# First-stage preparation of a two-block transformer kernel: parameters loaded in working layout, x on both partition halves

## The reference

```python
def rmsnorm(x, gain):
    y = x * rsqrt(mean(x * x) + EPS)
    return y * gain

def s5_mixer(u, lam, log_dt, b, c, d_skip, w_glu):      # 64 groups of 16 channels, 64 complex states each
    dt = exp(log_dt)
    a_bar = exp(lam * dt)
    b_bar = (a_bar - 1) / lam * b
    states = scan(a_bar, u @ b_bar)                     # along the 512 positions
    y = real(states @ c) + d_skip * u
    val, gate = split(gelu(y) @ w_glu)
    return val * sigmoid(gate)

def memory_cross_attention(h, m, w_q, w_kv, w_o):       # m = rmsnorm(mem) * g_mem
    kv = m @ w_kv                                       # 256 tokens, 256 key and 256 value columns
```

## Time and profile before

| what | us |
|---|---|
| median of three runs | 1854.55 |
| the profiled execution's own time | 1854.59 |
| its span, first to last instruction | 1852.8 |
| TensorE busy | 1814.2 |
| VectorE busy | 1144.7 |
| ScalarE busy | 838.7 |
| GpSimd busy | 734.2 |
| end of the load of x | 24.15 |
| first instruction of `rotate_in(0)` on VectorE | 53.29 |

### The profile page before, as it was taken

One profiled execution on the slowest core, in us unless ns is written; L12 is line 12 of the kernel. 1 busy time (PEld: TensorE's weight loads), 2 busy tenths in 40 slices (PEclk: granted clock), 3 DMA queues, 4 the chain that ended last, 5 costly groups with the idle time before them and its releaser, 6 DMA issues.

```text
span 1852.8 us, 24719 instructions
## 1 busy us (share of the span) xinstructions
PE 1814.2 (98%) x9727; PEld 1460.9 (79%) x9727; DVE 1144.7 (62%) x1684; ACT 838.7 (45%) x1361; POOL 734.2 (40%) x423
## 2 busy tenths in 40 slices
PE   7999999999999999999999999999999999999998
PEld 5778888888887688668888888887776768888886
DVE  8962435547475698853355474632636558787878
ACT  6852523333335435764323333353457464343444
POOL 1224343443424378543443443244245443324222
PEclk9999999999999999999999999999999999999999
DMA  6464452331412222003523414125120223415041
GB/s 169 89 149 101 117 156 69 114 114 46 137 46 75 69 92 91 24 24 109 165 68 108 120 46 137 46 83 153 57 69 24 80 92 113 128 54 169 13 137 46
DMA packets 200238, 171.29 MB, mean 92 GB/s; under 512 B 19258, under 2 KB 174346, under 8 KB 200058
## 3 DMA queue, kind: packets, MB, share of 16 engines
q1 hardware_dynamic: 197810, 165.93, 30.5%
q10 hardware_dynamic: 2312, 3.78, 0.6%
HBM read 162.58 MB, written 2.65 MB: 89 GB/s over the span
## 4 chain that ended last, share of the span: by engine, by line
PE 91%; DVE 3%; ACT 3%; issue 1%; DMA 1%; POOL 1%; SPq 0%; POOLq 0%; DVEq 0%; ACTq 0%
PE PS L2705 79%; PE PS L3067 2%; PE PS L3058 2%; PE PS L3077 2%; DMA xp<-in_x 1%; PE PS L2575 1%; PE PS L2618 1%; DVE taken L2393 1%; PE PS L3017 1%; PE PS L2984 0%; ACT probs_t L1481 0%; PE PS L2567 0%; PE PS L2627 0%; PE PS L2633 0%; ACT sq_junk L1138 0%
## 5 line engine op out<-in xcount | busy, mean ns | idle before, releaser
L783 POOL TENSOR_TENSOR w_lo<-raw,w_hi 128x2048 fp32r<-128x2048 f32 x92 | 430.1, 4675 | 604.2 <-ACT w_hi L1085 582.6
L2705 PE MATMUL PS<-xT_hi,w_hi 128*128 128x512 f32 (+1 forms) x1160 | 444.6, 383 | 3.1 <-DVE xT_lo L1922 2.0
L2705 PE MATMUL PS<-xT_lo,w_hi 128*128 128x512 f32 (+1 forms) x1160 | 441.8, 381 | 0.0
L2705 PE MATMUL PS<-xT_hi,w_lo 128*128 128x512 f32 (+1 forms) x1160 | 441.7, 381 | 0.0
L1085 ACT ACTIVATE w_hi<-raw 128x2048 fp32r<-128x2048 f32 x105 | 201.2, 1917 | 331.1 <-PE PS L2705 322.8
L2705 PEld LDWEIGHTS PS<-xT_hi,w_hi 128*128 128x128 f32 x1160 | 217.8, 188 | 50.0 <-issue 8.6
L2705 PEld LDWEIGHTS PS<-xT_lo,w_hi 128*128 128x128 f32 x1160 | 217.8, 188 | 42.2
L2705 PEld LDWEIGHTS PS<-xT_hi,w_lo 128*128 128x128 f32 x1160 | 217.9, 188 | 41.1
L790 POOL TENSOR_TENSOR w_lo<-dn_raw,w_hi 128x1024 fp32r<-128x1024 f32 (+1 forms) x46 | 123.4, 2703 | 262.5 <-ACT w_hi L1249 262.5
L2705 PE MATMUL PS<-w_hi,xT_hi 128*128 128x512 f32 (+1 forms) x560 | 220.2, 393 | 1.5 <-issue 1.5
L2705 PE MATMUL PS<-w_hi,xT_lo 128*128 128x512 f32 (+1 forms) x560 | 216.8, 387 | 0.0
(11 more groups left out here) (428 smaller groups left out, 2785.6 us busy)
## 6 DMA issues: line engine op xcount, KB each, us to landing
raw<-in_ffn_w_gate_up SPq DMA_DIRECT2D x88, 512.0 KB, 5.0
dn_raw<-in_ffn_w_down SPq DMA_DIRECT2D x22, 1024.0 KB, 7.6
raw<-in_w_up SPq DMA_DIRECT2D x32, 512.0 KB, 5.5
dn_raw<-in_w_down SPq DMA_DIRECT2D x16, 1024.0 KB, 8.0
raw<-in_dsa_w_in SPq DMA_DIRECT2D x28, 512.0 KB, 4.4
raw<-in_w_in SPq DMA_DIRECT2D x21, 512.0 KB, 4.9
raw<-in_s_w_glu SPq DMA_DIRECT2D x32, 256.0 KB, 4.9
raw<-in_dsa_w_o SPq DMA_DIRECT2D x8, 512.0 KB, 4.3
```

What stands on the lines that cost most here:

```text
L783: pool.tensor_tensor(w_lo[:, g % 2, :], raw[:, r % 2, :], f32(w_hi[:, g % 2, :]), ALU.subtract).then_inc(w_split, 1)
L2705: ins = mm(o, a if weights_stay else c, c if weights_stay else a, start=first and n == 0, stop=last and n == 2, skip_group_check=onto)
```

## The change

Parameters that were turned on the chip come from the host in the layout in which they are used (`laid_out`, a transposition and stacking of the arrays without arithmetic): lambda in one load, B as `b_n` and `b_s`, C as `c_n` and `c_s` (512 KB each), the gains as one 128x80 array, `w_kv` with 8 KB in a row per partition. The turns on TensorE and the copies on ScalarE for them go. Their signs change so that the state is kept conjugate: `rot` and `sign` change sign, `c_n` and `c_s` need no scaling, and `output_map` reads `pw_is` where it read `pw_i`.

x goes to 128 partitions, four positions of each chunk per partition (`xp[:, s, :]` for four `s`), in two loads of 64 partitions each. There are 4 squares of 128 partitions where there were 8 of 64, one inverse root in place of two, and all 8 scalings are ScalarE's, each still 64 partitions.

The order of the loads is log_dt, lambda, `mem`, `g_row`, B, x, the keys' half of `w_kv`, C, the values' half. ScalarE squares `mem` ahead of the two sines, and copies all of `memT` ahead of the squares of x. TensorE multiplies the first half of the keys ahead of the swap of B, and the rest behind it; the values' second half and `s5_lags(0)` move behind the turns of `u`. VectorE loses the three scalings, `pw_is` (now ScalarE's, behind the last square) and eight small instructions (memsets, the eighth power `r8` and the squared modulus of lambda, now GpSimd's), and makes `chunk_turns` ahead of `output_map(0)`. ScalarE makes `table(0)` behind `turned_rows`, where it stood ahead of `in_map_out(0)`.

```diff
 SyncE
-            for j, name in ((0, "s5_lambda_re"), (1, "s5_lambda_im")):
-                for half in range(2):
-                    sp.dma_start(nat_l[:, j, half, :], w[name][0]).then_inc(ld_lam, 16)
+            sp.dma_start(small[:, 1:3, :], w["s5_lambda"]).then_inc(ld_lam, 16)
+            sp.dma_start(mem[:, :, :], w["mem_2"].rearrange("(b p) d -> p b d", p=P)).then_inc(ld_mem, 16)
             sp.dma_start(g_row[:, :], w["norm_mix"][0:1, :]).then_inc(ld_rows, 16)
...
-            sp.dma_start(mem[:, :, :], w["mem_2"].rearrange("(b p) d -> p b d", p=P)).then_inc(ld_mem, 16)
-            sp.dma_start(xp[:, :, :], w["x"].rearrange("(c s) d -> c s d", s=CH)).then_inc(ld_x, 16)
...
+            for j, t in enumerate((b_n, b_s)):
+                sp.dma_start(t[:, :, :], w["s5_b"][:, j, :, :]).then_inc(ld_b, 16)
+            x_halves = w["x"].rearrange("(c f s) d -> f c s d", f=2, s=CQ)
+            for f in range(2):
+                sp.dma_start(xp[NC * f:NC * f + NC, :, :], x_halves[f]).then_inc(ld_x, 16)
+            sp.dma_start(w_kv[:, 0, :, :], w["w_xkv_2"][:, 0, :, :]).then_inc(ld_kvw, 16)
+            for j, t in enumerate((c_n, c_s)):
+                sp.dma_start(t[:, :, :], w["s5_c"][:, j, :, :]).then_inc(ld_c, 16)
+            sp.dma_start(w_kv[:, 1, :, :], w["w_xkv_2"][:, 1, :, :]).then_inc(ld_kvv, 16)
 GpSimd
+            pool.wait_ge(ld_lam, 16)
+            link(pool.tensor_tensor(small[:, 15, :], small[:, 1, :], small[:, 1, :], ALU.mult))
+            link(pool.tensor_tensor(small[:, 16, :], small[:, 2, :], small[:, 2, :], ALU.mult))
+            pool.tensor_tensor(small[:, 17, :], small[:, 15, :], small[:, 16, :], ALU.add).then_inc(const_set, 1)
...
+            pool.wait_ge(s5_ang, 1)
+            link(pool.tensor_tensor(r8[:, :], small[:, 8, :], small[:, 8, :], ALU.mult))
...
+            pool.wait_ge(s5_sq, CQ)
+            rsqrt(rstd[:, 0:CQ], ssq[:, 0:CQ], CQ, 1.0 / D).then_inc(s5_rstd, 1)
 ScalarE
-            square(0, 2)
-            mem_turned(0)
-            mem_turned(1)
-            square(2, 4)
-            mem_turned(2)
-            mem_turned(3)
+            for i in range(4):
+                mem_turned(i)
+            square(0, CQ - 1)
             act.wait_ge(s5_swap, 1)
             act.activation(b_s[:, 0:G // 2, :].rearrange("p g h -> p (g h)"), PS[:, 0, :], ACT.Copy)
             act.activation(b_s[:, G // 2:G, :].rearrange("p g h -> p (g h)"), PS[:, 7, :], ACT.Copy).then_inc(s5_bs, 1)
...
+            square(CQ - 1, CQ)
+            act.wait_ge(s5_pw, 1)
+            act.activation(pw_is[:, :, :], pw_i[:, :, :], ACT.Copy, scale=sign[:, 1:2]).then_inc(s5_pw_is, 1)
...
+            act.wait_ge(s5_rstd, 1)
+            for f in range(2):
+                for s in range(CQ):
+                    of = slice(NC * f, NC * f + NC)
+                    act.activation(u[:, :, CQ * f + s, :], xp[of, s, :].rearrange("p (g h) -> p g h", h=GH), ACT.Copy, scale=rstd[of, s:s + 1]).then_inc(s5_u, 1)
...
+            kv_copy(0)
             in_map_out(0)
-            turned_rows(0, 1)
-            kv_copy(0)
-            turned_rows(1, U_EARLY)
+            turned_rows(0, U_EARLY)
+            act.wait_ge(s5_u, CH)
+            table(0)
             lag_out(0)
 VectorE
+                if b == 0:
+                    dve.wait_ge(s5_bs, 1)
+                    dve.wait_ge(s5_pw_is, 1)
                 link(tt(in_im[:, :, :, :], over_k(b_s, b, CH), p_im, ALU.mult))
...
-            dve.wait_ge(s5_bs, 1)
-            dve.wait_ge(s5_skip, 1)
+            dve.wait_ge(s5_pw, 1)
             input_map(0)
-            dve.wait_ge(s5_nat_sb, 5)
+            chunk_turns()
+            dve.wait_ge(ld_c, 16 * 2)
             output_map(0)
-            chunk_turns()
-            dve.wait_ge(s5_rstd, 2)
-            for s in U_BY_DVE:
-                ts(u[:, :, s, :], xp[:, s, :].rearrange("p (g h) -> p g h", h=GH), rstd[0:NC, s:s + 1], None, ALU.mult).then_inc(s5_u_dve, 1)
             input_map(1)
 TensorE
+            def kv_keys(t):
+                for k in range(KT):
+                    if t == 0 and k % 2 == 0:
+                        pe.wait_ge(mem_t_sb, k // 2 + 1)
+                    ins = mm(PS[:, 4, MEM * t:MEM * t + MEM], w_kv[:, 0, k, P * t:P * t + P], memT[:, k, :], start=k == 0, stop=k == KT - 1)
+                return ins
+            pe.wait_ge(ld_kvw, 16)
+            kv_keys(0)
             pe.wait_ge(s5_bn, 1)
             pe.wait_ge(ld_rot, 16)
             for b in range(2):
                 ins = mm(PS[:, 7 * b, :], rot[:, 2 * P:3 * P], b_n[:, 32 * b:32 * b + 32, :].rearrange("p g h -> p (g h)"), start=True, stop=True)
             ins.then_inc(s5_swap, 1)
...
+            kv_keys(1).then_inc(kv_done, 1)
...
             s5_in_turn(0)
-            s5_lags(0)
-            kv_values(1).then_inc(kv_done, 1)
...
+            pe.wait_ge(s5_u, CH)
             u_turn(0, 3)
             pe.wait_ge(s5_int_sb, 1)
             u_turn(3, U_EARLY)
             pe.wait_ge(kv_sb, 1)
+            kv_values(1).then_inc(kv_done, 1)
+            pe.wait_ge(ld_c, 16 * 2)
+            s5_lags(0)
             pe.wait_ge(s5_ut_sb, 1)
             s5_in(0)
```

More of the change, by code:

```diff
@@ L768, in _ @@
             rsqrt(rstd[:, 32:34], ssq[:, 32:34], 2, 1.0 / D).then_inc(mem_rstd, 1)
-            for half in range(2):
-                rows = slice(CH // 2 * half, CH // 2 * half + CH // 2)
-                pool.wait_ge(s5_sq, rows.stop)
-                rsqrt(rstd[0:NC, rows], ssq[0:NC, rows], CH // 2, 1.0 / D, NC).then_inc(s5_rstd, 1)
+            pool.wait_ge(s5_ang, 1)
+            link(pool.tensor_tensor(r8[:, :], small[:, 8, :], small[:, 8, :], ALU.mult))
+            link(pool.tensor_tensor(r8[:, :], r8[:, :], r8[:, :], ALU.mult))
+            link(pool.tensor_tensor(r8[:, :], r8[:, :], r8[:, :], ALU.mult))
+            pool.wait_ge(s5_sq, CQ)
+            rsqrt(rstd[:, 0:CQ], ssq[:, 0:CQ], CQ, 1.0 / D).then_inc(s5_rstd, 1)
             def split_run(g0, n):
@@ L1775, in powers @@
                 link(tt(p, x, y[:, ::-1, :, :], ALU.mult))
-                link(tt(pw_i[:, :, lo + e:lo + e + n], p[:, 0, :, :], p[:, 1, :, :], ALU.add))
-            for lo, n, e in ((1, 1, 1), (1, 2, 2), (1, 4, 4)):
-                powers(lo, n, e)
-            link(ts(pw_is[:, :, :], pw_i[:, :, :], sign[:, 0:1], -1.0, ALU.mult, ALU.mult))
-            cycles = CH / (2 * np.pi)
-            link(ts(pt(10), pt(11), cycles, None, ALU.mult))
-            link(ts(pt(5).bitcast(I32), pt(11), cycles, None, ALU.mult))
+                return tt(pw_i[:, :, lo + e:lo + e + n], p[:, 0, :, :], p[:, 1, :, :], ALU.add)
+            link(powers(1, 1, 1))
+            link(powers(1, 2, 2))
+            powers(1, 4, 4).then_inc(s5_pw, 1)
             for side in range(2):
                 rows, gs = slice(GP * side, GP * side + GP), slice(G // 2 * side, G // 2 * side + G // 2)
-                link(stt(small[rows, 13, 0:G // 2], small[rows, 5, gs].bitcast(I32), -1.0, small[rows, 10, gs], ALU.mult, ALU.add))
+                link(stt(small[rows, 13, 0:G // 2], small[rows, 0, gs].bitcast(I32), -1.0, small[rows, 10, gs], ALU.mult, ALU.add))
             def chunk_turns():
@@ L1802, in output_map @@
                 gs = slice(GB * b, GB * b + GB)
-                p_re, p_im = (t[:, gs, 1:CH + 1].unsqueeze(3).broadcast_to([P, GB, CH, GH]) for t in (pw_r, pw_i))
+                p_re, p_im = (t[:, gs, 1:CH + 1].unsqueeze(3).broadcast_to([P, GB, CH, GH]) for t in (pw_r, pw_is))
                 if b >= 3:
@@ L2529, in _ @@
             ins.then_inc(s5_swap, 1)
-            pe.wait_ge(ld_c, 16 * 3)
-            for b in range(NB):
-                ins = tr(PS[:, 5 + b // 4, P * (b % 4):P * (b % 4) + P], nat_c[:, b, 0:2, :].rearrange("g a p -> g (a p)"), ident[:, :])
-            ins.then_inc(s5_nat, 1)
-            pe.wait_ge(mem_t_sb, 2)
-            for b in range(NB):
-                ins = tr(PS[:, 1 + b // 4, P * (b % 4):P * (b % 4) + P], nat_c[:, b, 1:3, :].rearrange("g a p -> g (a p)"), ident[:, :])
-            ins.then_inc(s5_nat, 1)
-            pe.wait_ge(mem_t_sb, 4)
-            pe.wait_ge(ld_kvw, 16)
-            for t in range(2):
-                for k in range(KT):
-                    ins = mm(PS[:, 4, MEM * t:MEM * t + MEM], w_kv[:, 0, k, P * t:P * t + P], memT[:, k, :], start=k == 0, stop=k == KT - 1)
-            ins.then_inc(kv_done, 1)
+            kv_keys(1).then_inc(kv_done, 1)
             def kv_values(m):
@@ L3302 @@
     arrays, w = {}, {}
-    for name, value in {**{n: inputs[n] for n in _INS}, **shape_constants()}.items():
+    for name, value in {**{n: inputs[n] for n in _INS}, **laid_out(inputs), **shape_constants()}.items():
         a = np.ascontiguousarray(value)
```

148 lines of the change are left out of this document (50 added, 98 removed).

## The result

The changed kernel takes 1859.3 us (median of 18 executions, 1856.35 to 1860.76), the kernel before, run beside it, 1854.55 us (18 executions, 1853.82 to 1857.02). The medians lie 4.75 us apart; the ratio is 1.0023, with a 95% interval of 1.0017 to 1.003, that is 3.2 to 5.6 us slower. The forecast was 1.3 us faster, and the result lies above the range (1851.2 to 1857.2). The profiled execution took 1860.76 us with a span of 1859.0, 6.2 us longer than the span before, and it is the slowest of the 18; the profile overstates the median's shift by 1.5 us.

The account below looks back on a forecast made before the run. It took TensorE's unbroken work, begun when `rotate_in(0)` can run, as the bound. Loads, keys, swap, scalings and tables summed to 52.0 us against 53.29, 1.3 us earlier: 1853.3 us, range 1851.2 to 1857.2.

Parts of the forecast that it names:

- half of the keys, half of 7.17: TensorE, from the keys' weights at 22.4: the first half of the keys was to end at 26.0 us.
- the second values, 3.72: TensorE behind the scalings: 3.7 us added ahead of the end of `s5_in(0)`, which came to 51.3, hidden by the tables.
- Its 6.0 us from before: TensorE from the end of the scalings, 46.4, to the end of `s5_in(0)`, 52.5, reused from the new scalings' end, 40.5.
- Loads: Start of the kernel: 219 GB/s for x in halves, 402 at full width; x there at 19.8, keys' weights at 22.4.
- 2.6 us (my choice): Assumed time at which the first loads' data begin to flow, with `mem` there at 7.6 us.
- Rival 2: Weights at 251 GB/s, landing 27.2, hold up TensorE: 1858.1 us, 1860.4 with crowded root; 0.07 beyond 3.7 us later.
- the part to which 0.07 was given: Whole kernel: rival 2 beyond 3.7 us later than before, counted as slower than what a measurement can tell from no change.
- two thirds of the way: Upper end of the forecast range, 1857.2 us, placed two thirds of the way to rival 2's end.
- Rival 1: The `mem` turn decides, weights landing by 20.6: everything 1.8 us earlier, tables at 50.2, 1851.5 us; chance 0.15.
- Rival 3: VectorE decides, ScalarE's arm over 3.7 us shorter than summed: `rotate_in(0)` at 48.3, 5.0 us earlier, 1849.6 us; chance 0.10.
- ScalarE's sum: ScalarE from the last square to the tables: inverse root, eight scalings to 40.5, five `uT` to 44.6, `table(0)` to 47.7.
- One for one: Behind `rotate_in(0)` nothing is altered, so its shift, 1.3 us earlier, was carried unchanged to the end.

Follow-up runs that it names:

- the control: Kernel before the change with one added wait, so TensorE starts the keys only behind the sixth square of x: 1860.82 us, ratio 1.0034.
- the profiled execution without fills: Changed kernel with x in one load, two squares of x between the copies of `mem`, `pw_is` between scalings, no filling matmuls: median 1851.67 us; this execution was the fastest.
- x in one load and the order, with fills: Changed kernel with x in one load, two squares between the copies of `mem`, `pw_is` between scalings, and filling matmuls in TensorE's pauses: 1851.62 us.

## Why the prediction was wrong

**The step that failed** is the price of TensorE's work behind the new waits. The sum took "half of the keys, half of 7.17", the turns of u and "the second values, 3.72" from rows at a granted clock of 1.00 and set them behind two pauses that it could see itself (20.6 to 22.4, and from the first input turn to the end of the scalings). Its sentence that the removed turns "are costed at nothing of their own: with the order above their place is empty time" took that empty time as free. The runs showed 6.32, 4.53 and 5.90 us in place of 3.6, 2.73 and 3.72, at a clock of 0.50; with the first pause filled the keys took 3.72, and a pause put into the kernel before made its keys 1.7 us longer. What is shown is the price of a pause. That the removed turns as such had kept the clock up is not shown: without them, one load of x or the swap first also brings the time back to 1854 us.

The error at `rotate_in(0)` is 58.56 - 52.0 = 6.6 us, in the profiled execution:

| term | forecast | measured | adds |
|---|---|---|---|
| keys' weights there | 22.4 | 24.84 | 2.4 |
| first half of the keys | 3.6 | 6.32 | 2.7 |
| swap to end of the scalings | 14.5 | 14.0 | -0.5 |
| turns of u to end of `s5_in(0)` | 10.8 | 13.3 | 2.5 |
| from there to `rotate_in(0)` | 0.7 | 0.1 | -0.6 |

The terms add up to 6.5, the 6.6 but for rounding. The loads are 2.4 of these and the half clock on the keys 2.7. The fourth row hides a second error: the half clock took 1.8 us on the turns of u and 2.2 on the values, 4.0 in all, but the forecast's 10.8 held some 1.5 us too much. Its 6.0 us from before began at 46.4, when TensorE was still at the second values until 47.8, and the second values were then added once more.

- **Loads.** The rates were right: 209 GB/s for x in halves (219 taken), 412 for the weights (402 taken). The start was not. The squares of `mem` begin at 8.8, not 7.6, so 1.2 us was late from the "2.6 us (my choice)": the windows have 55 GB/s from 2 to 4 us and 312 from 4 to 6. x was 2.7 us late (22.5) and the keys' weights 2.4; where the second half of that delay comes from was not separated.
- **Rival 2** named the right place: TensorE held up by the keys' weights, and slower from a landing at 23.7 on. With 24.84 it gives `rotate_in(0)` at 54.4 and 1855.7 us. Its price was too small by 4.2 us, which is the half clock's 6.7 less the slack and the 1.5 us of above. The result, 4.75 us slower than before, lies in the part to which 0.07 was given. Its own mechanism did not come true, though: the rate did not drop to 251 GB/s, and TensorE was idle for 3.74 us ahead of the keys, where its sign was over 5. The upper end of the range, "two thirds of the way", doesn't come out of the rival's times either: from 1853.3 that is 1856.5 towards 1858.1, or 1858.0 towards 1860.4.
- **Rival 1** is settled by the load in one piece. The halves did not flow together, and where x came at full width, as that rival wanted, the kernel took 1853.9 us, not 1851.5. (With the 0.5 us to signal, its x would be there at 15.4, not 15.0.)
- **Rival 3**, VectorE decides, fell for this change; its time, 48.3, is exactly what VectorE needs once x and the order let it (48.28 to 48.42 in three runs).
- **ScalarE's sum** was right: scalings 8.55 us (8.5 taken), GpSimd's root 0.19 and 1.02 (0.31 and 1.29 taken). The five `uT` took 3.9 us, not 2.6, paced by TensorE's slow turns; this brought the table copies to 57.74.
- **One for one** held within 0.9 us: +5.3 at `rotate_in(0)`, +6.2 at the end. The rest came by the table copies of the third batch, for which VectorE waited 1.49 us at 78.93, and 0.41 at 72.58 before. In the control it was +5.5 and +5.4.

How much of the loss is the clock is known only in part. Filling the first pause gave 1.9 us of the median and filling both 2.5. With fills in all pauses of the first 45 us it was 2.2, and the three executions of that run with a mean clock of 0.999 lay 4.3 below the changed kernel's median. One load of x gave 5.4 us and the old order 5.2, but both also did away with the half clock on the keys in the profiled execution. So these figures overlap with the clock's and do not add up. The 4.3 us is the nearest to late weights at full clock throughout: it leaves 0.7 us over the kernel before, where the forecast's sum with the measured landing gives 1.2 (1855.7). But it rests on three executions picked by their clock, none of them profiled.

What stays open: why the clock falls in some executions of one kernel and not in others, and what beyond a pause's length decides. Pauses of 3.81 and 3.09 us in the kernel before, 3.20 with the swap first, and 2.46 and 1.29 in two kernels with fills went by without a fall, and so did the first 8.13 us of the changed kernel; pauses of 1.04 to 1.98 us were followed by one. These short pauses all stood ahead of the turns of u, forty matmuls of 64 rows, and the clock fell during those matmuls; where the pause there was filled to the end, they ran at full clock. No run here isolates that.

## What to carry to other kernels

When a change takes work from TensorE or makes it wait, price the pause twice: the pause, and the work behind it at both durations that the profile shows for that line (here 3.62 and 6.32 us for sixteen matmuls). Look then for what hides it; a half clock beside another engine's list costs nothing, as the profiled execution without fills shows. If you fill a pause, look at what is left of it (1.04 and 1.25 us were followed by a fall, 0.85 and 2.46 elsewhere were not) and follow where the wait goes next. Rather remove its cause: one load over all partitions and the swap ahead of the late weights were each worth more than any fill alone.

## What the runs showed of the hardware

- The granted clock falls also while TensorE is busy, 0.8 to 2.6 us after a pause of 1.0 to 2.0 us has ended: at about 40.5 us behind 1.04 (x in one load and a fill), 38.6 behind 1.98 (the order without fills), 44.5 behind 1.25 (both pauses filled), 39.7 behind 1.74 (the swap first). It did so at 50.7 too, behind 2.89 us (x in one load and the order, with fills). The times are worked out from the windows' mean clocks.
- It stayed at 0.50 for some 7 us (23 to 30 in the changed kernel, 33 to 40 in the control) or 10 us (44 to 54). TensorE was busy for 5.3, 3.4 and 8.9 us of these stretches. The Trainium skill ("TensorE: Matmul & The Clock Gate", section "HAM oscillation — how this bites in real kernels") tells of a TensorE that waits for loads and starts each burst of work at the lower clock; the changed kernel's first pause, a wait for the keys' weights, agrees, with 6.32 against 3.62 us.
- Executions of one kernel scatter in part with their mean clock: in the series with x in one load and a fill the three at 0.995 took 1858 us, but those at 0.998 and 0.999 took anything from 1851.6 to 1855.7. Where fills left no pause above 1.3 us from 12 us on, all eight were at 0.999 and took 1849.4 to 1851.2 us.
- Two loads of 64 partitions moved 209 GB/s, one of 128 moved 413, in the window from 12 to 20 us of the same kernel but for that load; with x in one load the window holds the keys' weights too, from about 16 us; 12 to 14 and 14 to 16 us, x alone, had 434 and 377.
